# Two blocks of a small language model on one core: pool products moved behind the compressed scores, recurrence outputs turned into four PSUM banks

## Chip, cores and metric

One core of one Trainium2 chip runs the whole program. The metric is device time in microseconds (us), the median of several runs; lower is better. TensorE (PE in the rows, its weight loads PEld) multiplies, VectorE (DVE), ScalarE (ACT) and GpSimd (POOL) work on elements, SyncE (SP) issues most transfers.

## What is computed

A sequence of 512 tokens of width 1024 passes through two blocks, all in fp32. Cut to what matters here:

```python
# first block
u, q, kv, nsa_g, merge_g = split(rms_norm(x) @ w_in)
pooled_g = window_mean(u_g, 2, 4, 8, 16) - u_g               # four groups g of 128 columns
y_pool = concat(pooled_g @ pool_w[g]) * pool_scale @ w_pool_out
kc, vc = compress_blocks(kv)                                 # 31 compressed keys and values
p_cmp = masked_softmax(q @ kc * scale)                       # then attention over all branches
x = x + (gate_pool * y_pool + gate_nsa * y_nsa) @ w_out      # and a gated feed-forward
# second block
o = gated_delta_rule(q, k, v, g, beta)                       # recurrence, 4 heads, 8 chunks of 64 tokens
oa = rmsnorm(o, gdn_norm_w) * silu(z)
ob = chunk_band_attention(qb, kb, vb, rel_bias)
x = x + (sigmoid(ga) * (oa @ w_branch_a) + sigmoid(gb) * (ob @ w_branch_b)) @ w_out
```

## The kernel before, in words

Activations lie transposed in SBUF, features on the 128 partitions, the 512 tokens along the free axis. Every weight tile is a *chunk* of 128 x 1024 values. It is loaded into one of two slots of `w_raw` by SyncE (`load`, L584), cast by ScalarE to `w_hi` (L790), and its rest `w_lo` is made by VectorE or, in the stretches that the change touches, by GpSimd in four pieces (`low_pieces`, L561). A product is then three matmuls of 512 columns for each 128 rows of weights: `w_hi` with `h_hi`, `w_hi` with `h_lo`, `w_lo` with `h_hi` (L1686 to L1688).

The order on each engine is written out by hand; semaphores join the engines. Long serial passages, the compressed attention of block 1 and the recurrence of block 2, give TensorE little to do. Into their gaps the program puts pieces of a projection that is wanted only later: `fill(step, n)` on TensorE runs so many *pieces* (a quarter of a chunk, six matmuls) as a plan gives that step. Two chunks are in PSUM banks 0 and 1 at a time. When a chunk's four pieces are done, VectorE's `serve(step, n)` scales it into `stage` (L1164) and SyncE stores it (L588); ScalarE's and GpSimd's `serve` of the same step make the weights of the chunk two further on. Each engine reaches its `serve` in its own program order. The pieces that matter here:

```python
# step: pieces run by TensorE; VectorE's, ScalarE's and GpSimd's serve of the step runs up to chunk first_piece // 4
compress 3: 24      compress 4: 25      scores 0: 26-29     scores 1: 30-33
out 0: 73-75   out 1: 76-78   out 2: 79-81   out 3: 82-84   turn 0: 85-86   turn 1: 87-88
```

So the last piece of out 3, number 84, is the first of chunk 21. ScalarE casts that chunk in `serve("out", 3)`, which stands behind its loop over the four heads:

```python
for h in range(GH):
    act.wait_ge(f_dve, 4 + 2 * h)
    act.activation(oa_hi[:, h, :], oa[:, h % 2, :], ACT.Copy).then_inc(oa_h, 1)
...
act.wait_ge(oa_l, GH)
act.dma_start(rel[:, :, :], diagonals(rel_dram)).then_inc(rel_loaded, 16)
serve("out", 3)
```

PSUM has eight banks: ACC (0, 1) for filling, BS (2, 3), BT (4, 5), BO (6, 7). In the compressed stage TensorE multiplies four pooled groups by `pool_w`; ScalarE makes `yp_hi` of each (L1009), VectorE `yp_lo` (L1429). Before the change groups 2 and 3 (counted from 0) reuse the banks of groups 0 and 1 and wait for their `yp_lo`; the scores (L1961) follow behind them and one filling piece. In the out stage TensorE transposes four heads of `o_nat` (printed as p2a), 4 transposes a head, through the helper `turn` (L1785) into BT and BT+1 in alternation, so that heads 2 and 3 wait until VectorE has read heads 0 and 1 into `oa` (L1654). VectorE's loop takes one head at a time: two halves of `oa`, a wait for ScalarE's `oa_hi` (L1114), the subtraction `oa_lo` (L1141).

Of the kernel before, what the change touches and what calls it, by code (L numbers as in the profile page):

```python
# [25 lines left out]
ACT = mybir.ActivationFunctionType  # L26
AXX = mybir.AxisListType.X

P = 128
# [8 lines left out]
GH = 4  # L38
# [162 lines left out]
def two_blocks(nc, t_in, out):  # L201
# [10 lines left out]
    with ctx:  # L212
# [54 lines left out]
        p1 = area("p1", [P, 15, T], F32, 0)  # L267
# [8 lines left out]
        pool_w = area("pool_w", [P, 4, P], F32, 82)  # L276
# [20 lines left out]
        yp_hi = area("yp_hi", [P, 4, T], F32R, 0)  # L297
        yp_lo = area("yp_lo", [P, 4, T], F32R, 16)
# [47 lines left out]
        o_nat = p2a[:, 4:8, :].rearrange("p c (h d) -> p c h d", h=GH)  # L346
        o_sq = p2a[:, 8:12, :].rearrange("p c (h d) -> p c h d", h=GH)
        oa = area("oa", [P, 2, T], F32, 34)
# [17 lines left out]

        banks = ctx.enter_context(nc.psum_tensor("banks", [P, 8, T], F32))
        ACC, BS, BT, BO = 0, 2, 4, 6
        POOLED = (BS + 1, BT + 1)

        def bank(n, shape=None):
            v = banks[:, n, :]
            return v.rearrange("p (a b) -> p a b", a=shape) if shape else v
# [58 lines left out]
        pooled = sem("pooled")  # L432
        pool_mul = sem("pool_mul")
        yp_h, yp_l = sem("yp_h"), sem("yp_l")
# [54 lines left out]

        LATE_BANK = (1, 1)  # L490
        KEY_BANK = (BO, BS)

        block = ctx.enter_context(nc.Block())

# [11 lines left out]
        POOL_STEPS = [5 + gi for gi in range(4)]  # L506
# [64 lines left out]
        def wait(eng, s, value):  # L571
            if not isinstance(value, int) or value > 0:
                eng.wait_ge(s, value)
# [211 lines left out]
        def _(act):  # L785
# [218 lines left out]
            act.activation(kc_tmp[:, 1, :], kc_tmp[:, 1, :], ACT.Exp, scale=-0.5).then_inc(c_act, 1)  # L1004
            serve("compress", 3)

            for gi in range(4):
                act.wait_ge(pool_mul, gi + 1)
                act.activation(yp_hi[:, gi, :], bank(POOLED[gi % 2]), ACT.Copy, scale=param("pool_scale", gi, 1))\  # L1009
                    .then_inc(yp_h, 1)  # L1010
            serve("compress", 4)

            act.wait_ge(s_dve, 6)
            act.activation(cmp_s[:, :, :, :, :], cmp_s[:, :, :, :, :], ACT.Exp, scale=DH ** -0.5).then_inc(s_act, 1)
            serve("scores", 0)
            serve("scores", 1)
            act.wait_ge(blk_zero, 1)
            for r in range(8):
# [120 lines left out]
        def _(dve):  # L1139
# [284 lines left out]
            for half in range(2):  # L1424
                dve.tensor_tensor(kc_two[rows(half), half, :], kc_tmp[rows(half), 2, :], kc_tmp[rows(half), 3, :],
                                  ALU.add).then_inc(c_dve, 1)
            for gi in range(4):
                dve.wait_ge(yp_h, gi + 1)
                dve.scalar_tensor_tensor(yp_lo[:, gi, :], bank(POOLED[gi % 2]), param("pool_scale", gi, 1),  # L1429
                                         yp_hi[:, gi, :], ALU.mult, ALU.subtract).then_inc(yp_l, 1)  # L1430
            serve("compress", 4)

            flat = cmp_s[:, :, :, :, :].rearrange("p a b c n -> p (a b c) n")
# [14 lines left out]
            serve("scores", 0)  # L1448
            dve.wait_ge(s_act, 1)
            dve.tensor_reduce(cmp_red[:, 1, :], flat, AXX, ALU.add).then_inc(s_dve, 1)  # L1450
            serve("scores", 1)
            dve.wait_ge(s_dve, 7)
            dve.reciprocal(cmp_red[:, 2, :], cmp_red[:, 1, :]).then_inc(s_dve, 1)
# [192 lines left out]
            def in_pairs(row, side):  # L1646

                return row.rearrange("p (c two t) -> p c two t", c=NT, two=2)[:, :, side, :]

            for h in range(GH):  # L1650
                dve.wait_ge(f_pe, h + 1)
                wait(dve, oa_l, h - 1)
                for side in range(2):
                    dve.scalar_tensor_tensor(in_pairs(oa[:, h % 2, :], side), in_pairs(bank(BT + h % 2), 1 - side),  # L1654
                                             param("gdn_gain"), in_pairs(p2a[:, 12 + h, :], side),
                                             ALU.mult, ALU.mult).then_inc(f_dve, 1)
                dve.wait_ge(oa_h, h + 1)
                sub(oa_lo[:, h, :], oa[:, h % 2, :], oa_hi[:, h, :]).then_inc(oa_l, 1)
                if h == 1:
                    serve("out", 2)  # L1660
# [17 lines left out]
        def _(pe):  # L1678
# [105 lines left out]
            def turn(dst, src, n=P, last=None):  # L1784
                return pe.transpose(dst, src, ident[0:n, 0:n])  # L1785
# [122 lines left out]
                elif n == 2:  # L1908
                    add_parts()
            rotate(5)  # L1910
            pe.wait_ge(c_act, 2)
            for v in range(2):
                for k in range(NT):
                    mm = turn(banks[:, BO + v, k * P:(k + 1) * P], p1[:, VS + v, k * P:(k + 1) * P])
                mm.then_inc(turned[0], 1)
                fill("turn", v)
# [21 lines left out]
            pe.wait_ge(c_act, 3)  # L1938
            pe.matmul(banks[:, BS, 0:NCMP], halves, kc_tmp[:, 0, :], start=True, stop=True).then_inc(c_pe, 1)

            for gi in range(2):
                pe.wait_ge(pooled, sum(POOL_STEPS[:gi + 1]))
                pe.matmul(bank(POOLED[gi % 2]), pool_w[:, gi, :], p1[:, gi, :], start=True, stop=True)\
                    .then_inc(pool_mul, 1)
            fill("compress", 3)
            pe.wait_ge(c_dve, 1)
            pe.matmul(banks[:, BT, 0:NCMP], const("rot"), kc_t[:, :], start=True, stop=True).then_inc(c_pe, 1)
            for gi in range(2, 4):
                pe.wait_ge(pooled, sum(POOL_STEPS[:gi + 1]))
                pe.wait_ge(yp_l, gi - 1)  # L1950
                pe.matmul(bank(POOLED[gi % 2]), pool_w[:, gi, :], p1[:, gi, :], start=True, stop=True)\
                    .then_inc(pool_mul, 1)
            fill("compress", 4)

            pe.wait_ge(c_dve, 5)
            pe.wait_ge(n_sum, 6)
            pe.wait_ge(yp_l, 3)
            for i2 in range(2):
                for n in range(8):
                    i, j, at_ = 2 * i2 + n // 4, n % 4, n * 2 * NCMP  # L1960
                    mm = pe.matmul(banks[:, BS + i2, at_:at_ + 2 * NCMP], p1[:, 4 + j, i * P:(i + 1) * P],  # L1961
                                   kc_two[:, :, :].rearrange("p a b -> p (a b)"), start=True, stop=True)
                mm.then_inc(s_pe, 1)
            fill("scores", 0)
            fill("scores", 1)
            pe.wait_ge(s_dve, 12)
# [118 lines left out]
            for c in range(NCH):  # L2085
# [21 lines left out]
                                   u_new[rs, slot, h, :], start=c == 0 and h == 0, stop=True,  # L2107
                                   skip_group_check=True)
                mm.then_inc(r_o, 1)
            fill("out", 0)  # L2110
            fill("out", 1)
            pe.wait_ge(f_dve, 2)
            for h in range(GH):
                wait(pe, f_dve, 2 * h if h >= 2 else 0)
                for p in range(NT):
                    mm = turn(banks[:, BT + h % 2, p * P:(p + 1) * P], o_nat[:, p, h, :])
                mm.then_inc(f_pe, 1)
            fill("out", 2)
            fill("out", 3)
            for v in range(4):  # L2120
                fill("turn", v)
                pe.wait_ge(qkv_in["v"], 16)
                wait(pe, v_copied[1], v - 1)
                for k in range(NT):
                    mm = turn(banks[:, BO + v % 2, k * P:(k + 1) * P], p2b[:, 8 + v, k * P:(k + 1) * P])
                mm.then_inc(turned[1], 1)
# [130 lines left out]
```

## Time and profile before

| | us |
|---|---|
| median of 3 runs (1584.78 to 1585.86) | 1585.39 |
| the profiled execution's own time | 1585.66 |
| its span, first to last instruction | 1583.9 |
| TensorE busy in the span | 1547.2 |

The rows below come from that one execution; their times count from the start of its span. In a timeline row the first number is the start, the second the duration of the row's instructions together, `x8` their number, and the bracket the idle time of the engine just before with what ended it. Matmuls overlap, so a row's duration is longer than the distance to the next start. The clock column PEclk is the share of 2.4 GHz that was granted: 1.00 is 2.4 GHz, 0.50 is 1.2 GHz.

### The profile page before, as it was taken

What the parts mean: (1) busy time and instruction counts of PE and PEld (TensorE: products, weight loads), DVE (VectorE), ACT (ScalarE), POOL (GpSimd) and SP (SyncE); (2) the same over time, 40 slices, a digit from 0 to 9 for tenths busy, and PEclk for the clock granted to TensorE, in tenths of its full rate; (3) what the DMA queues carried; (4) which work ended last, traced back from release to release, by engine and by line L of the source; (5) the groups of instructions that cost most, each with busy time, mean ns of one, the idle gap of its engine ahead of it and who ended that gap; (6) DMA issues with size and microseconds to landing.
All of it is one profiled execution on the core that took longest, in us unless ns stands there. A gap on an engine that the chain in (4) does not pass through costs nothing.

```text
span 1583.9 us, 21470 instructions
## 1 busy us (share of the span) xinstructions
PE 1547.2 (98%) x7712; PEld 1237.7 (78%) x7712; DVE 896.5 (57%) x1437; ACT 571.4 (36%) x874; POOL 207.8 (13%) x263
## 2 busy tenths in 40 slices
PE   8999999999999999999999999999999999999997
PEld 5876676788888888888787778766788888888885
DVE  6128567565666665333863652346566788887233
ACT  4234456544323333223324413236544332332221
POOL 1548112100000000000002362232100000000000
PEclk9999999999999999999999999999999999999999
DMA  7423112342322323232222241251342232223221
GB/s 245 148 88 107 61 54 72 109 147 93 107 93 93 106 92 114 92 104 77 82 104 99 101 131 54 75 205 67 143 144 94 93 105 94 93 98 121 97 91 71
DMA packets 58100, 164.72 MB, mean 104 GB/s; under 512 B 11936, under 2 KB 12200, under 8 KB 57904
## 3 DMA queue, kind: packets, MB, share of 16 engines
q1 hardware_dynamic: 52784, 158.07, 28.9%
q10 hardware_dynamic: 5248, 5.74, 1.2%
q8 instruction: 43, 0.70, 0.2%
q14 instruction: 25, 0.20, 0.0%
HBM read 148.83 MB, written 14.96 MB: 103 GB/s over the span
## 4 chain that ended last, share of the span: by engine, by line
PE 89%; DVE 5%; DMA 2%; ACT 2%; issue 1%; ACTq 0%; POOL 0%; SPq 0%; DVEq 0%; POOLq 0%
PE banks L1686 26%; PE banks L1688 26%; PE banks L1687 26%; PE banks L1785 2%; PE banks L1796 2%; PE banks L1825 2%; DMA w_raw<-in_w_in 1%; PE banks L2102 0%; PE banks L2081 0%; ACT w_hi L790 0%; PE banks L2093 0%; PE banks L2023 0%; PE banks L2066 0%; DMA w_raw<-in_w_mix 0%; PE banks L1992 0%
## 5 line engine op out<-in xcount | busy, mean ns | idle before, releaser
L1686 PE MATMUL banks<-h_hi,w_hi 128*128 128x512 f32 x1312 | 531.9, 405 | 9.2 <-POOL w_lo L561 4.5
L1688 PE MATMUL banks<-h_hi,w_lo 128*128 128x512 f32 x1312 | 513.3, 391 | 0.0
L1687 PE MATMUL banks<-h_lo,w_hi 128*128 128x512 f32 x1312 | 513.2, 391 | 0.0
L790 ACT ACTIVATE w_hi<-w_raw 128x1024 fp32r<-128x1024 f32 (+1 forms) x226 | 249.3, 1103 | 474.5 <-PE banks L1688 412.6
L1686 PEld LDWEIGHTS banks<-h_hi,w_hi 128*128 128x128 f32 x1312 | 247.6, 189 | 95.9 <-issue 28.9
L1687 PEld LDWEIGHTS banks<-h_lo,w_hi 128*128 128x128 f32 x1312 | 247.8, 189 | 53.3 <-issue 5.1
L1688 PEld LDWEIGHTS banks<-h_hi,w_lo 128*128 128x128 f32 x1312 | 247.3, 188 | 53.0
L553 DVE TENSOR_TENSOR w_lo<-w_raw,w_hi 128x1024 fp32r<-128x1024 f32 (+1 forms) x168 | 217.9, 1297 | 82.6 <-ACT w_hi L790 82.5
L561 POOL TENSOR_TENSOR w_lo<-w_raw,w_hi 128x256 fp32r<-128x256 f32 x232 | 177.3, 797 | 380.2 <-ACT w_hi L790 380.0
L1686 PE MATMUL banks<-act_hi,w_hi 128*128 128x512 f32 x352 | 136.9, 389 | 0.0
L1687 PE MATMUL banks<-act_lo,w_hi 128*128 128x512 f32 x352 | 136.9, 389 | 0.0
L1688 PE MATMUL banks<-act_hi,w_lo 128*128 128x512 f32 x352 | 136.9, 389 | 0.0
L1164 DVE TENSOR_TENSOR t_raw<-banks,rms_inv 128x512 f32<-128x512 f32 x66 | 45.6, 691 | 78.3 <-PE banks L1688 70.9
L1187 DVE TENSOR_TENSOR X<-X,banks 128x512 f32<-128x512 f32 (+1 forms) x32 | 22.0, 687 | 98.6 <-PE banks L1688 98.6
L1686 PEld LDWEIGHTS banks<-act_hi,w_hi 128*128 128x128 f32 x352 | 66.1, 188 | 13.8
L1688 PEld LDWEIGHTS banks<-act_hi,w_lo 128*128 128x128 f32 x352 | 66.1, 188 | 13.7
L1687 PEld LDWEIGHTS banks<-act_lo,w_hi 128*128 128x128 f32 x352 | 66.1, 188 | 13.7
L862 ACT ACTIVATE act_hi<-t_gate 128x512 f32 (+1 forms) x44 | 27.8, 632 | 133.8 <-DVE t_gate L1256 133.8
L895 ACT ACTIVATE at_p<-at_sm,cols 128x128 f32<-128x128 f32 (+2 forms) x96 | 52.9, 552 | 61.3 <-PE banks L1785 42.7
L747 POOL MEMSET x_inv<- 128x2048 f32 x1 | 1.8, 1813 | 518.5 <-DVE p2a L1164 518.5
L859 ACT ACTIVATE t_gate<-t_gate 128x512 f32<-128x512 f32 x44 | 27.9, 633 | 95.1 <-DVE t_gate L1232 95.1
L1686 PE MATMUL banks<-mix_hi,w_hi 128*128 128x512 f32 x128 | 49.8, 389 | 0.0
(291 smaller groups left out, 1739.1 us busy)
## 6 DMA issues: line engine op xcount, KB each, us to landing
w_raw<-in_w_up SPq DMA_DIRECT2D x88, 512.0 KB, 3.5
w_raw<-in_w_fill SPq DMA_DIRECT2D x44, 512.0 KB, 3.5
w_raw<-in_w_down SPq DMA_DIRECT2D x32, 704.0 KB, 4.0
late_scratch<-stage SPq DMA_DIRECT2D x44, 256.0 KB, 2.0
w_raw<-in_w_mix SPq DMA_DIRECT2D x16, 512.0 KB, 4.3
sg<-late_scratch SPq DMA_DIRECT2D x16, 512.0 KB, 3.8
w_raw<-in_w_out SPq DMA_DIRECT2D x16, 512.0 KB, 3.5
w_raw<-in_w_in SPq DMA_DIRECT2D x13, 512.0 KB, 3.5
```

Source lines behind the costliest of these rows:

```text
L553: eng.tensor_tensor(w_lo[:, c.slot, 0:kt * P], w_raw[:, c.slot, 0:kt * P], w_hi[:, c.slot, 0:kt * P], ALU.subtract).then_inc(lo_ready, PIECES)
L561: eng.tensor_tensor(w_lo[:, c.slot, cols], w_raw[:, c.slot, cols], w_hi[:, c.slot, cols], ALU.subtract).then_inc(lo_ready, 1)
L790: act.activation(w_hi[:, c.slot, 0:kt * P], w_raw[:, c.slot, 0:kt * P], ACT.Copy)\
L859: act.activation(t_gate[:, j, :], t_gate[:, j, :], ACT.Silu).then_inc(silu_done[b], 1)
L895: act.activation(a.p[:, s % 2, half, off:off + w], a.sm[:, half, off:off + w], ACT.Exp, bias=a.nbias[:, c:c + 1], scale=DH ** -0.5, accum_ ...
L1164: return dve.tensor_tensor(dst, src, rms_inv[:, :], ALU.mult)
L1686: pe.matmul(dst, w_h, hi[:, kr, :], start=first and n == 0, stop=False)
L1687: pe.matmul(dst, w_h, lo[:, kr, :], start=False, stop=False)
L1688: mm = pe.matmul(dst, w_l, hi[:, kr, :], start=False, stop=last and n == len(ks) - 1)
L1785: return pe.transpose(dst, src, ident[0:n, 0:n])
L1796: mm = pe.matmul(banks[:, BS + half, off:off + w], q_tile(j)[rows(half), i * P:(i + 1) * P], k_tile(j, b)[rows(half), 0:w], start=True, st ...
L1825: mm = pe.matmul(banks[rows(half), BO + j % 2, i * P:(i + 1) * P], v_tile(j, b, half, k), a.pt[u % 2][half][:, off + k * P:off + (k + 1) * P],
```

## The change

In the compressed stage the pool products 2 and 3 go to banks BO and BO+1 of their own, behind the scores, and no longer wait for `yp_lo`; the scores wait for one `yp_lo` instead of three. ScalarE's and VectorE's shares of these two groups move behind the Exp and the sum of the compressed softmax. Before that, the first of the two value turns no longer waits for `hid_t`. In the out stage the four heads are turned into four banks without a wait between them, the filling step out 2 moves in front of the turns, and the value turns that use BO and BO+1 next wait until all heads are read. The order on GpSimd and SyncE, and the plan of pieces, stay.

```diff
-        POOLED = (BS + 1, BT + 1)
+        POOLED = (BS + 1, BT + 1, BO, BO + 1)
+        TURNED = (BT, BT + 1, BO, BO + 1)
...
# ScalarE
-            for gi in range(4):
+            def pooled_high(gi):
                 act.wait_ge(pool_mul, gi + 1)
...
+            for gi in range(2):
+                pooled_high(gi)
             serve("compress", 4)
             act.wait_ge(s_dve, 6)
             act.activation(cmp_s[:, :, :, :, :], cmp_s[:, :, :, :, :], ACT.Exp, scale=DH ** -0.5).then_inc(s_act, 1)
             serve("scores", 0)
+            for gi in range(2, 4):
+                pooled_high(gi)
             serve("scores", 1)
# VectorE
+            for gi in range(2):
+                pooled_low(gi)
             serve("compress", 4)
...
             dve.tensor_reduce(cmp_red[:, 1, :], flat, AXX, ALU.add).then_inc(s_dve, 1)
+            for gi in range(2, 4):
+                pooled_low(gi)
             serve("scores", 1)
...
-                    dve.scalar_tensor_tensor(in_pairs(oa[:, h % 2, :], side), in_pairs(bank(BT + h % 2), 1 - side),
+                    dve.scalar_tensor_tensor(in_pairs(oa[:, h % 2, :], side), in_pairs(bank(TURNED[h]), 1 - side),
# TensorE
-            pe.wait_ge(c_act, 2)
             for v in range(2):
+                if v:
+                    pe.wait_ge(c_act, 2)
...
             pe.matmul(banks[:, BT, 0:NCMP], const("rot"), kc_t[:, :], start=True, stop=True).then_inc(c_pe, 1)
-            for gi in range(2, 4):
-                pe.wait_ge(pooled, sum(POOL_STEPS[:gi + 1]))
-                pe.wait_ge(yp_l, gi - 1)
-                pe.matmul(bank(POOLED[gi % 2]), pool_w[:, gi, :], p1[:, gi, :], start=True, stop=True)\
-                    .then_inc(pool_mul, 1)
             fill("compress", 4)
             pe.wait_ge(c_dve, 5)
             pe.wait_ge(n_sum, 6)
-            pe.wait_ge(yp_l, 3)
+            pe.wait_ge(yp_l, 1)
...
                 mm.then_inc(s_pe, 1)
+            pe.wait_ge(c_act, 4)
+            for gi in range(2, 4):
+                pool_product(gi)
             fill("scores", 0)
             fill("scores", 1)
...
-            fill("out", 0)
-            fill("out", 1)
+            for n in range(3):
+                fill("out", n)
             pe.wait_ge(f_dve, 2)
             for h in range(GH):
-                wait(pe, f_dve, 2 * h if h >= 2 else 0)
                 for p in range(NT):
-                    mm = turn(banks[:, BT + h % 2, p * P:(p + 1) * P], o_nat[:, p, h, :])
+                    mm = turn(banks[:, TURNED[h], p * P:(p + 1) * P], o_nat[:, p, h, :])
                 mm.then_inc(f_pe, 1)
-            fill("out", 2)
             fill("out", 3)
             for v in range(4):
                 fill("turn", v)
                 pe.wait_ge(qkv_in["v"], 16)
+                pe.wait_ge(f_dve, 2 + 2 * GH)
```

## Rows read from the trace of the kernel before

**Rows 1.** The page: engines over the span, then the last chain by engine.

```profile
PE 1547.2 (98%) x7712; PEld 1237.7 (78%) x7712; DVE 896.5 (57%) x1437; ACT 571.4 (36%) x874; POOL 207.8 (13%) x263
...
PE 89%; DVE 5%; DMA 2%; ACT 2%; issue 1%; ACTq 0%; POOL 0%; SPq 0%; DVEq 0%; POOLq 0%
```

**Rows 2.** TensorE's waits over the span: total us, times, longest us.

```profile
PE banks L1951 <- DVE yp_lo L1429: 2.4, 1, 2.4
...
PE banks L1785 <- ACT hid_t L979: 1.3, 1, 1.3
```

**Rows 3.** Three stretches: length, busy us per engine (instructions), clock, DMA share, GB/s.

```profile
29.80:36.62 6.82, 5.87 (x14) 4.61 (x15) 6.07 (x9) 1.50 (x2) 4.07 (x6) 0.50 0.37 113
...
159.46:162.87 3.41, 3.41 (x7) 1.93 (x6) 1.33 (x2) 1.37 (x2) 0.00 (x0) 0.50 0.21 79
...
1036.69:1040.10 3.41, 3.37 (x10) 2.89 (x11) 2.03 (x4) 1.26 (x2) 0.00 (x0) 0.50 0.38 144
```

**Rows 4.** TensorE in order of time, compressed stage.

```profile
152.49 1.96 PE L1943 MATMUL banks<-p,pool_w 128*128 128x512 f32 x4
153.89 0.79 PE L1686 MATMUL banks<-h_hi,w_hi 128*128 128x512 f32 x1
...
155.80 0.41 PE L1947 MATMUL banks<-kc_t,consts 128*128 128x31 f32 x2
158.61 2.92 PE L1951 MATMUL banks<-p,pool_w 128*128 128x512 f32 x4 [2.40 <-DVE yp_lo L1429]
...
163.43 3.68 PE L1961 MATMUL banks<-kc_two,p 128*128 128x62 f32 x32
166.92 0.48 PE L1686 MATMUL banks<-h_hi,w_hi 128*128 128x512 f32 x1
...
177.93 1.03 PE L1785 MATMUL banks<-consts,cmp_s 128*31 128x128 f32 x8
```

**Rows 5.** VectorE in order of time, the same stage.

```profile
157.72 1.41 DVE L1429 SCALAR_TENSOR_TENSOR yp_lo<-banks,params,yp_hi 128x512 fp32r<-128x512 f32 x2
...
174.65 1.69 DVE L1465 TENSOR_TENSOR cmp_s<-cmp_s,cmp_red 128x992 f32<-128x992 f32 x1
```

**Rows 6.** ScalarE in order of time, the same stage.

```profile
154.00 1.25 ACT L1009 ACTIVATE yp_hi<-banks,params 128x512 fp32r<-128x512 f32 x2
...
170.36 1.03 ACT L1014 ACTIVATE cmp_s<-cmp_s 128x992 f32<-128x992 f32 x1 [8.11 <-DVE cmp_s L1141]
```

**Rows 7.** TensorE in order of time, out stage.

```profile
1031.62 0.39 PE L1688 MATMUL banks<-h_hi,w_lo 128*128 128x512 f32 x1
1032.75 1.09 PE L1785 MATMUL banks<-consts,p2a 128*128 128x128 f32 x8 [0.74 <-DVE p2a L1643]
...
1037.50 0.78 PE L1686 MATMUL banks<-h_hi,w_hi 128*128 128x512 f32 x1
...
1045.65 0.39 PE L1686 MATMUL banks<-h_hi,w_hi 128*128 128x512 f32 x1
```

**Rows 8.** All engines in order of time, out stage: casts and low weights.

```profile
1031.40 3.94 POOL L561 TENSOR_TENSOR w_lo<-w_raw,w_hi 128x256 fp32r<-128x256 f32 x4 [3.18 <-ACT w_hi L790]
...
1042.98 1.06 ACT L790 ACTIVATE w_hi<-w_raw 128x1024 fp32r<-128x1024 f32 x1 [1.29 <-DVE oa_lo L1141]
...
1044.12 5.76 POOL L561 TENSOR_TENSOR w_lo<-w_raw,w_hi 128x256 fp32r<-128x256 f32 x8 [8.78 <-ACT w_hi L790]
```

**Rows 9.** VectorE in order of time, out stage.

```profile
1032.61 0.68 DVE L1164 TENSOR_TENSOR stage<-banks,rms_inv 128x512 f32<-128x512 f32 x1
1033.44 0.88 DVE L1654 SCALAR_TENSOR_TENSOR oa<-banks,params,p2a 128x256 f32<-128x256 f32 x2
...
1035.02 0.88 DVE L1141 TENSOR_TENSOR oa_lo<-oa,oa_hi 128x512 fp32r<-128x512 f32 x1 [0.70 <-ACT oa_hi L1114]
...
1041.73 0.69 DVE L1141 TENSOR_TENSOR oa_lo<-oa,oa_hi 128x512 fp32r<-128x512 f32 x1 [0.70 <-ACT oa_hi L1114]
```

**Rows 10.** DMA issues in the out stage: KB each, us to landing.

```profile
rel<-rel_scratch ACTq DMA_DIRECT2D x1, 2048.0 KB, 13.8
```

More of the change, by code:

```diff
@@ L1005, in _ @@
             serve("compress", 3)
-            for gi in range(4):
+            def pooled_high(gi):
                 act.wait_ge(pool_mul, gi + 1)
-                act.activation(yp_hi[:, gi, :], bank(POOLED[gi % 2]), ACT.Copy, scale=param("pool_scale", gi, 1))\
+                act.activation(yp_hi[:, gi, :], bank(POOLED[gi]), ACT.Copy, scale=param("pool_scale", gi, 1))\
                     .then_inc(yp_h, 1)
+            for gi in range(2):
+                pooled_high(gi)
             serve("compress", 4)
@@ L1426, in _, with pooled_low @@
                                   ALU.add).then_inc(c_dve, 1)
-            for gi in range(4):
+            def pooled_low(gi):
                 dve.wait_ge(yp_h, gi + 1)
-                dve.scalar_tensor_tensor(yp_lo[:, gi, :], bank(POOLED[gi % 2]), param("pool_scale", gi, 1),
+                dve.scalar_tensor_tensor(yp_lo[:, gi, :], bank(POOLED[gi]), param("pool_scale", gi, 1),
                                          yp_hi[:, gi, :], ALU.mult, ALU.subtract).then_inc(yp_l, 1)
+            for gi in range(2):
+                pooled_low(gi)
             serve("compress", 4)
@@ L1939, in _, with pool_product @@
             pe.matmul(banks[:, BS, 0:NCMP], halves, kc_tmp[:, 0, :], start=True, stop=True).then_inc(c_pe, 1)
+            def pool_product(gi):
+                pe.wait_ge(pooled, sum(POOL_STEPS[:gi + 1]))
+                pe.matmul(bank(POOLED[gi]), pool_w[:, gi, :], p1[:, gi, :], start=True, stop=True)\
+                    .then_inc(pool_mul, 1)
             for gi in range(2):
-                pe.wait_ge(pooled, sum(POOL_STEPS[:gi + 1]))
-                pe.matmul(bank(POOLED[gi % 2]), pool_w[:, gi, :], p1[:, gi, :], start=True, stop=True)\
-                    .then_inc(pool_mul, 1)
+                pool_product(gi)
             fill("compress", 3)
@@ L1947, in _ @@
             pe.matmul(banks[:, BT, 0:NCMP], const("rot"), kc_t[:, :], start=True, stop=True).then_inc(c_pe, 1)
-            for gi in range(2, 4):
-                pe.wait_ge(pooled, sum(POOL_STEPS[:gi + 1]))
-                pe.wait_ge(yp_l, gi - 1)
-                pe.matmul(bank(POOLED[gi % 2]), pool_w[:, gi, :], p1[:, gi, :], start=True, stop=True)\
-                    .then_inc(pool_mul, 1)
             fill("compress", 4)
@@ L1963, in _ @@
                 mm.then_inc(s_pe, 1)
+            pe.wait_ge(c_act, 4)
+            for gi in range(2, 4):
+                pool_product(gi)
             fill("scores", 0)
```

## The prediction

> **What bounds the kernel.** I read the page first. TensorE is busy 98% of the span and carries 89% of the chain that ended last [rows 1]; no other engine comes near. So a change can only win where TensorE stands still or where its clock is low, and it loses wherever it makes TensorE stand still longer. The second view is TensorE's waits over the whole span: the pool products on L1951 wait 2.4 us for `yp_lo`, and a turn waits 1.3 us for `hid_t` [rows 2]. The third is the granted clock: three stretches at 0.50, that is at 1.2 GHz instead of 2.4. One lies in the start, which the diff leaves alone, one right behind the wait on L1951, one inside the turning of the recurrence outputs [rows 3]. Both later ones lie where the diff works. The fourth view is the order of time on each engine in those two stretches [rows 4 to 10]; there the reader is to see for each gap which instruction ended it, and what had to run before that instruction.
>
> **Unit prices.** Filling matmuls at full clock: 48 run from 166.92 to 177.93 [rows 4], 0.229 us each. A fill piece has six, 1.38 us. At half clock 14 matmuls are busy for 5.87 us [rows 3], 0.42 us each, so each loses 0.19 us: about 1.5 us in a busy stretch of 3.41 us and 2.7 us over the 5.87 us. Two pool products take 1.40 us to the next start, and the first fill behind them is 0.4 us longer than usual [rows 4]: 1.7 us of path.
>
> **Edit 1, the first value turn without its wait.** The 1.3 us wait for `hid_t` [rows 2] goes; everything TensorE issues next up to L1947 moves up by it. What is late next is L1947 at 155.80, which needs `kc_t`, and that stands on VectorE behind `pooling` 2 and 3, which pace themselves. The same 1.3 us therefore come back as a wait in front of L1947. From below this edit is worth nothing; from above it cannot be worth more than 1.3 us. I take 0, because VectorE is busy with the pooling up to `kc_t` and only its small waits for TensorE could close.
>
> **Edit 2, products 3 and 4 behind the scores.** Before: L1947 at 155.80, a gap until the first `yp_lo` is out, products from 158.61 (2.92 us, mostly at half clock), one fill piece at half clock, scores at 163.43, next filling at 166.92 [rows 4]. After: the fill piece "compress 4" runs right behind L1947 (156.0 to 157.4; its weights are the second piece of a chunk whose first piece has just run). The scores then wait for `kc_two` and for one `yp_lo` instead of three. The `yp_lo` pair starts at 157.72 and takes 1.41 us [rows 5], so the first is out at about 158.5, and product 3 did start at 158.61 on just that event [rows 4]. The scores start there, 4.8 us earlier than at 163.43. They take 163.43 to 166.92, 3.5 us; then come both products, 1.7 us, whose new banks BO and BO+1 have been read long before. Filling begins at 158.6 + 3.5 + 1.7 = 163.8 instead of 166.92: **-3.1 us**. In this are 1.2 us of the 2.4 us wait, saved by the fill piece, and the loss of the half-clock stretch. If the clock falls here too, 1.5 us of that go.
>
> Does it last? The compressed turns need the last multiplication into `cmp_s`, which ended at 174.65 + 1.69 = 176.34, while TensorE came at 177.93 [rows 4, 5]: 1.6 us to spare. That chain starts with the scores and so moves up 4.8 us, and gets two insertions: behind the Exp (ending 165.5 + 1.03) ScalarE takes the two `yp_hi`, 1.25 us [rows 6], in front of the weight cast for scores 1; VectorE takes both `yp_lo`, 1.41 us [rows 5], behind the sum. Allowing VectorE its wait for ScalarE, some 0.2 us, it ends near 176.3 - 4.8 + 1.6 = 173.1. TensorE comes at 163.8 + 11.0 = 174.8. Nothing waits. I bound the term by -2.0 (two thirds kept) and -4.0 (0.9 us gained by edit 1 as well).
>
> **Edit 3, the turning of the recurrence outputs.** Before, TensorE finishes filling at about 1031.85, turns heads 0 and 1 at 1032.75, waits for `oa` before heads 2 and 3, and fills again from 1037.50, at half clock until 1040.10 [rows 3, 7]. Six pieces follow: out 2 and out 3. The last of the six opens chunk 21 and starts at 1045.65 [rows 7]. It is the place that decides. Its low weights come from GpSimd at 1044.12, from a ScalarE cast at 1042.98 [rows 8], which ScalarE only reaches behind all four `oa_hi`, behind the wait for all four `oa_lo` and behind the issue of the `rel` DMA. VectorE makes `oa_lo` one head after the other: head 0 from 1033.44, its subtraction from 1035.02, the last head's from 1041.73 to 1042.42 [rows 9]. Four banks don't shorten this: VectorE waits for ScalarE's `oa_hi` inside each head, and that wait stays.
>
> After: the first piece of out 2 runs 1031.85 to 1033.2. The second opens chunk 20, whose bank is free after VectorE's eviction, 1032.61 + 0.68 [rows 9], and whose low weights are under way from 1031.40, four pieces in 3.94 us [rows 8]; so it runs almost without a gap, and the third ends at 1036.05. Only now come the turns. A group of four is read some 0.7 us after it begins (eight began at 1032.75, the first `oa` at 1033.44) [rows 7, 9], so VectorE's chain begins at 1036.7 instead of 1033.44: **3.3 us late**. Head 0's subtraction was 0.2 us longer (0.88 us) than the last one's (0.69 us) [rows 9] and I don't count that again, so the chain ends at 1042.42 + 3.1 = 1045.5. The cast follows at 1046.1, GpSimd 1.14 us later at 1047.2, its first piece (5.76 us for eight, 0.72) at 1047.9 [rows 8]. TensorE has meanwhile turned all heads (16 at 1.09 us for eight: 1.9 us at most, to 1038.0) and run two pieces (to 1040.7). It then **stands still for about 7 us** in front of the piece that opens chunk 21, until 1048.0: **+2.35 us** against 1045.65. The removed waits between 1031.85 and 1037.50 are thus collected in one place and lengthened. Bounds: 2.0 if the turns are read as soon as four of them can be done, 3.0 if the opening of chunk 20 slips by the 0.7 us of a GpSimd piece.
>
> The GpSimd row beside head 0 is where a page bears on the 0.2 us. The `oa_lo` subtraction took 0.88 us there, beside GpSimd's casts, and 0.69 us for the last head [rows 8, 9]. The Trainium skill, "GPSIMD Engine Reference", section "1. Specifications", says that VectorE instructions with two SBUF inputs contend with GpSimd; the trace agrees, and as GpSimd would be through its four pieces before the moved chain begins its subtractions, the term would be 2.35 by that and 2.55 by the row as it stands.
>
> Behind that wait the clock is at half again, as it was after the shorter waits in both stretches and in the start [rows 3]. Price between 1.5 us (one stretch like 1036.69 to 1040.10) and 2.7 us (the start's). A pause of 7 us is nearer to the start's, so I take **+2.3 us**. The Trainium skill, "TensorE: Matmul & The Clock Gate", section "HAM oscillation — how this bites in real kernels", speaks against the change here: bursts of matmuls parted by long waits are slowed at the start of each burst. By it this term stands; without it the sum would be -0.75 us.
>
> What comes behind is moved with TensorE. The `rel` DMA is issued 3.1 us later, at about 1045.6, and landed in 13.8 us [rows 10]: 1059.4. Attention's first mask needs it only behind nine pieces and four value turns, at 1048.0 + 12.4 us or later still, by the half clock and the turns. The slack is small but positive. The added wait of the value turns for ten `f_dve` is over when the last `oa` is, before 1045; two fill pieces lie in between.
>
> **Sum.** -3.1 + 2.35 + 2.3 = +1.55 us on the profiled execution's own 1585.66 us: 1587.2. That execution lies 0.27 us above the median of 1585.39, so I forecast **1586.9 us**. A change within 0.2% (3.2 us) can't be told from none in a measurement of this kernel.
>
> **Rivals.**
> *Forecast (0.66):* gain and loss nearly cancel; terms at their bounds give -4.0 + 2.0 + 1.5 = -0.5 to -2.0 + 3.0 + 2.7 = +3.7, mostly within 0.2%; 0.05 of this is slower.
> *Edit 3 gains too (0.06):* the piece that opens chunk 21 is not held, TensorE goes through at 1040.7, 5 us earlier than before, and the end is at 1585.4 - 3.1 - 5.0 = 1577.3. For it: before, the piece waited for nothing. Against it: its weights were there (1044.84) only 0.8 us before it began, and the cast's place behind the four heads is unchanged.
> *The compressed softmax comes late (0.13), the side of slower:* the `yp` copies inserted on ScalarE and VectorE push the last `cmp_s` behind TensorE's arrival. It decides once they cost 1.7 us more than I allow (173.1 against 174.8); if it eats the 3.1 us, the result is 1585.4 + 4.65 = 1590.0. For it: both engines are strictly serial there. Against it: 4.8 us of head start.
> *The clock falls in the compressed stage as well (0.15):* TensorE still pauses there, in front of L1947 and of the scores. +1.5 us: 1588.4, on the edge of 0.2%; I count 0.04 of it as slower.
>
> So: faster 0.08 (the second rival and 0.02 for what I don't see), slower 0.05 + 0.13 + 0.04 = 0.22, no difference 0.70. The range 1584.0 to 1589.8 leaves out the second rival below and part of the late softmax above.
>
> **What would show it.** Right: scores 4 to 5 us earlier against L1947, no half clock behind them; the largest wait of the page that is new is TensorE's for `w_lo` from GpSimd, about 7 us, right behind the turns, followed by half clock; `oa` chain unchanged in length and 3 us later. Wrong: no such wait, or TensorE waiting in front of the compressed turns, or filling behind the scores not 3 us earlier.

## The result, and the profile after

The change makes the kernel slower: 1594.59 us (median of 5 runs, 1590.88 to 1595.84) against 1585.39 us beside it (5 runs, 1584.59 to 1587.89), ratio 1.0051, 95% interval 1.0038 to 1.0064. That is 9.2 us, where the forecast was +1.5 us and the range ended at 1589.8. (The ratio goes by all executions; the quotient of the two medians would be 1.0058.)

The page of the changed kernel, engines over the span and the last chain by engine, answers to [rows 1]:

```profile
PE 1551.3 (97%) x7712; PEld 1241.4 (78%) x7712; DVE 898.5 (56%) x1437; ACT 571.1 (36%) x874; POOL 207.8 (13%) x263
...
PE 89%; DVE 5%; DMA 2%; ACT 2%; issue 1%; ACTq 0%; POOL 0%; SPq 0%; DVEq 0%; POOLq 0%
```

TensorE is still the bound, and it is busy 4.1 us longer for the same 7712 instructions. So a part of the loss is not waiting but slower matmuls. TensorE's waits in the changed kernel, the two longest (us in total, times, longest), answer to [rows 2]:

```profile
PE banks L1697 <- POOL w_lo L562: 11.7, 3, 7.3
PE banks L1962 <- DVE kc_t L1419: 3.6, 1, 3.6
```

The first was forecast. The second was forecast as 1.3 us. The waits of 2.4 us for `yp_lo` in front of the products and of 1.3 us for `hid_t` are gone. Three stretches of the changed kernel (length, busy us per engine, clock), answering to [rows 3]:

```profile
153.01:159.85 6.84, 3.20 (x14) 2.21 (x13) 6.50 (x13) 1.13 (x2) 4.20 (x4) 0.99 0.20 72
159.85:170.09 10.24, 10.13 (x38) 8.01 (x37) 4.32 (x8) 0.00 (x0) 0.00 (x0) 0.50 0.22 78
1047.31:1057.55 10.24, 5.68 (x14) 4.47 (x15) 2.58 (x5) 2.63 (x3) 5.56 (x8) 0.50 0.79 277
```

In each of the two stages 10.24 us run at 1.2 GHz, where it was 3.41 us before. In the compressed stage TensorE is busy for 10.13 of them, and the clock still stays down.

**Where the 9.1 us of the two spans (1593.0 against 1583.9) arise.** Two distances serve for all kernels below, each read from one profiled execution. The *compressed distance* runs from the moment when TensorE is ready for the first value turn to the first of the compressed turns: 136.32 (137.66 less its wait of 1.34) to 177.93 before, 41.61 us; 136.60 to 181.39 after, 44.79 us. The *out distance* runs from VectorE's multiplication into `p2a` in front of the heads to the first mask of attention: 1030.40 to 1061.71 before, 31.31 us; 1034.07 to 1070.63 after, 36.56 us. So the compressed stage brings +3.18, the out stage +5.25, and everything else together +0.7.

TensorE of the changed kernel in order of time, both stages, answers to [rows 4, 7]:

```profile
136.60 0.60 PE L1796 MATMUL banks<-consts,p 128*128 128x128 f32 x4
...
158.35 0.41 PE L1962 MATMUL banks<-kc_t,consts 128*128 128x31 f32 x2 [3.64 <-DVE kc_t L1419]
...
160.62 7.06 PE L1971 MATMUL banks<-kc_two,p 128*128 128x62 f32 x32
167.47 3.20 PE L1955 MATMUL banks<-p,pool_w 128*128 128x512 f32 x4
...
181.39 1.03 PE L1796 MATMUL banks<-consts,cmp_s 128*31 128x128 f32 x8
...
1039.96 1.91 PE L1796 MATMUL banks<-consts,p2a 128*128 128x128 f32 x16
...
1051.87 0.79 PE L1697 MATMUL banks<-h_hi,w_hi 128*128 128x512 f32 x1 [7.27 <-POOL w_lo L562]
```

The 32 score matmuls take 7.06 us instead of 3.68, all of them at half clock. What made TensorE wait for `kc_t` is read on VectorE and GpSimd. VectorE of the changed kernel in order of time (`pooling` 2 and `kc_t`):

```profile
140.97 3.39 DVE L522 TENSOR_TENSOR pool_pad<-pool_pad 128x512 f32<-128x512 f32 x3
144.40 4.30 DVE L526 TENSOR_SCALAR pool_pad<-pool_pad 128x496 f32<-128x496 f32 x1
...
158.05 0.25 DVE L1419 SCALAR_TENSOR_TENSOR kc_t<-banks,params,kc_tmp 128x31 f32<-128x31 f32 x1
```

GpSimd of the changed kernel over the same time:

```profile
136.49 8.47 POOL L562 TENSOR_TENSOR w_lo<-w_raw,w_hi 128x256 fp32r<-128x256 f32 x8
144.91 3.52 POOL L742 MEMSET pc_t<- 128x4096 f32 x1
```

The same instructions of the kernel before, which no row ahead shows, GpSimd and then VectorE in order of time (the row at 153.58 is the same scaling in `pooling` 3, while GpSimd stands idle):

```profile
136.04 4.11 POOL L561 TENSOR_TENSOR w_lo<-w_raw,w_hi 128x256 fp32r<-128x256 f32 x4
140.94 4.31 POOL L561 TENSOR_TENSOR w_lo<-w_raw,w_hi 128x256 fp32r<-128x256 f32 x4 [0.79 <-ACT w_hi L790]
145.19 3.52 POOL L741 MEMSET pc_t<- 128x4096 f32 x1
```

```profile
143.81 0.84 DVE L525 TENSOR_SCALAR pool_pad<-pool_pad 128x496 f32<-128x496 f32 x1
...
145.31 0.69 DVE L527 TENSOR_TENSOR p<-pool_pad,p 128x512 f32<-128x512 f32 x1
...
146.95 2.04 DVE L519 COPY pool_pad<-p 128x512 f32<-128x512 f32 x1
...
153.58 0.42 DVE L525 TENSOR_SCALAR pool_pad<-pool_pad 128x496 f32<-128x496 f32 x1
...
155.50 0.25 DVE L1413 SCALAR_TENSOR_TENSOR kc_t<-banks,params,kc_tmp 128x31 f32<-128x31 f32 x1
```

Before, the TENSOR_SCALAR of `pooling` 2 (its scaling by 1/w) was through 0.54 us before GpSimd's zeroing of `pc_t` began, and only the COPY that opens `pooling` 3 met it. After, the zeroing has moved 0.28 us forward and the TENSOR_SCALAR 0.59 us back (both counted from the start of their span), and they meet: 4.30 us instead of 0.84. Seen piece by piece, the TENSOR_SCALAR began before the change during the third of GpSimd's four low-weight pieces (143.19 to 144.38) and after it during the last of eight (143.78 to 144.96), right behind which the zeroing stands. Each of the two ends just behind the zeroing (148.70 against 148.43; before 148.99 against 148.71). The rows of the out stage stand further down, with edit 3.

### The profile page after: what moved, and what is told of

Its sections match the earlier page's. It is cut to its first block, busy times and chain, and to the rows that moved or that the text cites. A ratio compares the mean times of both kernels' runs of the same rounds, so it can differ in the third digit from the quotient of the medians.

```text
span 1593.0 us, 21471 instructions
## 1 busy us (share of the span) xinstructions
PE 1551.3 (97%) x7712; PEld 1241.4 (78%) x7712; DVE 898.5 (56%) x1437; ACT 571.1 (36%) x874; POOL 207.8 (13%) x263
## 4 chain that ended last, share of the span: by engine, by line
PE 89%; DVE 5%; DMA 2%; ACT 2%; issue 1%; ACTq 0%; POOL 0%; SPq 0%; DVEq 0%; POOLq 0%
PE banks L1697 26%; PE banks L1699 25%; PE banks L1698 25%; PE banks L1796 2%; PE banks L1807 2%; PE banks L1836 2%; DMA w_raw<-in_w_in 1%; PE banks L2115 0%; PE banks L2094 0%; ACT w_hi L791 0%; PE banks L2106 0%; PE banks L2036 0%; PE banks L2079 0%; PE banks L1971 0%; DVE pool_pad L522 0%
```

## The experiments

The table gives each kernel's median, its ratio to the kernel before run beside it (with the 95% interval), and of the profiled execution the compressed distance, the length of the half-clock stretch in that stage, and the out distance, all in us. The medians of the kernel before beside them were 1585.36 (first four), 1584.90 (next four) and 1584.66 (last two). A median stands for 5 to 12 executions, a distance for one, and whole spans of single executions mislead: that of e1_alone is 1.4 us shorter than that of the kernel before (1582.5 against 1583.9), although its median is longer, because its first value turn happens to come 3.50 us earlier (132.82 against 136.32).

| kernel | median | ratio | compressed | at half clock | out |
|---|---|---|---|---|---|
| before | 1585.39 | | 41.61 | 3.4 | 31.31 |
| after | 1594.59 | 1.0051 [1.0038, 1.0064] | 44.79 | 10.2 | 36.56 |
| e1_alone | 1588.02 | 1.0015 [1.0005, 1.0025] | 44.01 | 6.8 | 31.24 |
| e2_alone | 1582.43 | 0.9986 [0.9977, 0.9995] | 38.59 | 0 | 30.67 |
| e3_alone | 1590.50 | 1.0032 [1.0020, 1.0043] | 41.65 | 3.4 | 36.16 |
| e12 | 1587.27 | 1.0011 [0.9999, 1.0023] | 44.69 | 10.2 | 30.72 |
| e1_late_zero | 1581.63 | 0.9985 [0.9975, 0.9994] | 38.11 | 0 | 30.70 |
| zero_late | 1585.06 | 0.9995 [0.9986, 1.0004] | 41.22 | 3.4 | 30.69 |
| e3_early | 1583.54 | 0.9988 [0.9979, 0.9998] | 41.59 | 3.4 | 29.07 |
| all_mended | 1581.58 | 0.9983 [0.9971, 0.9994] | 36.75 | 0 | 30.40 |
| after_zero_late | 1586.57 | 1.0006 [0.9998, 1.0015] | 40.06 | 6.8 | 35.55 |
| e12_zero_late | 1580.78 | 0.9972 [0.9960, 0.9984] | 36.78 | 0 | 31.30 |

### 1. Each edit alone, and the first two together

**e1_alone**, the kernel before with edit 1:

```diff
-            pe.wait_ge(c_act, 2)
             for v in range(2):
+                if v:
+                    pe.wait_ge(c_act, 2)
```

> The kernel before with edit 1 alone: the first value turn doesn't wait for hid_t. Theory: the wait of 1.3 us goes, but ScalarE's cast and GpSimd's zeroing of pc_t (3.52 us) come a little earlier and now lie over VectorE's TENSOR_SCALAR of pooling 2, which takes over 4 us as in the changed kernel (0.84 before), so kc_t comes about 2 us later and TensorE waits some 3.6 us in front of L1947: +2 to +3.5 us, the upper end if the clock falls for longer. Rival (mine in the prediction): the time comes back as an equal wait, 0 us; the late kc_t of the changed kernel was then the chance of one execution, and kc_t here comes 20 us after the first value turn as before.

Measured: +2.7 us, compressed distance +2.40. VectorE of this kernel in order of time shows the stretched instruction with the two other edits absent; the second fence is TensorE:

```profile
140.62 4.31 DVE L525 TENSOR_SCALAR pool_pad<-pool_pad 128x496 f32<-128x496 f32 x1
```

```profile
154.59 0.53 PE L1948 MATMUL banks<-kc_t,consts 128*128 128x31 f32 x2 [3.66 <-DVE kc_t L1413]
156.86 3.75 PE L1952 MATMUL banks<-p,pool_w 128*128 128x512 f32 x4 [1.73 <-DVE yp_lo L1429]
```

Edit 1 by itself is the source of the wait for `kc_t`.

**e2_alone**, the kernel before with the diff's POOLED, `pooled_high`, `pooled_low` and `pool_product` parts:

```diff
-            for gi in range(2, 4):
...
-                pe.wait_ge(yp_l, gi - 1)
...
             fill("compress", 4)
...
-            pe.wait_ge(yp_l, 3)
+            pe.wait_ge(yp_l, 1)
...
+            for gi in range(2, 4):
+                pool_product(gi)
```

> The kernel before with edit 2 alone: products 3 and 4 behind the scores. Theory: kc_t comes when it did before, TensorE pauses only 1.2 us in front of the scores, the clock stays at full level through the scores, and filling behind them starts 3.1 us earlier: -3 us. Rival: products and scores in this order let the clock fall whatever happened before, scores take some 7 us at half clock as in the changed kernel instead of 3.5: +0.5 to +1 us.

Measured: -2.9 us, compressed distance -3.02. TensorE of this kernel in order of time, then its stretch from 152 to 175:

```profile
156.03 0.41 PE L1960 MATMUL banks<-kc_t,consts 128*128 128x31 f32 x2
...
158.87 3.75 PE L1969 MATMUL banks<-kc_two,p 128*128 128x62 f32 x32 [0.94 <-DVE yp_lo L1434]
162.46 1.94 PE L1953 MATMUL banks<-p,pool_w 128*128 128x512 f32 x4
```

```profile
152.00:175.00 23.00, 22.06 (x108) 16.99 (x107) 16.99 (x28) 6.42 (x10) 7.34 (x10) 1.00 0.27 92
```

The scores start 2.84 us behind the matmul on `kc_t` (7.63 before, [rows 4]), at full clock.

**e3_alone**, the kernel before with TURNED and the moved `fill("out", 2)`:

```diff
-            fill("out", 0)
-            fill("out", 1)
+            for n in range(3):
+                fill("out", n)
...
-                    mm = turn(banks[:, BT + h % 2, p * P:(p + 1) * P], o_nat[:, p, h, :])
+                    mm = turn(banks[:, TURNED[h], p * P:(p + 1) * P], o_nat[:, p, h, :])
...
-            fill("out", 2)
```

> The kernel before with edit 3 alone: four turns into four banks, out 2 in front of them. Theory: TensorE waits about 7.3 us for the low weights of chunk 21 behind two pieces of out 3, and resumes at half clock for 3 to 6 us: +4.6 to +5.5 us. Rival: part of the loss in the changed kernel's out stage comes from the earlier stages' shift (where the DMAs and casts meet); then this one alone costs less than 3 us.

Measured: +5.1 us, out distance +4.85, with the same wait for `w_lo`. TensorE of this kernel in order of time:

```profile
1048.76 0.80 PE L1687 MATMUL banks<-h_hi,w_hi 128*128 128x512 f32 x1 [7.26 <-POOL w_lo L562]
```

**e12**, the change without its TURNED part (the diff of e1_alone and that of e2_alone together).

> Edits 1 and 2 together, out stage as before. Theory (the two act on each other): edit 1's late kc_t makes TensorE wait 3.6 us, the clock falls, and the scores that edit 2 puts right behind keep it at half for longer than one stretch: +2 to +4 us, more than the sum of the two alone (near -1). Rival: the parts add up, -1 us, and the rest of the 9 us comes from the out stage.

Measured: +1.9 us in the median (its interval just reaches no difference), compressed distance +3.08, where the parts add up to 2.40 - 3.02 = -0.62. So in these executions 3.7 us come from having both; in the medians it is 1.9 against 2.7 - 2.9 = -0.2, that is 2.1. The stage of this execution is that of the changed kernel: a wait of 3.65 us, 10.24 us at half clock, and on TensorE:

```profile
161.31 7.06 PE L1970 MATMUL banks<-kc_two,p 128*128 128x62 f32 x32
```

In e1_alone the clock fell as well, but was back up before the scores, which took 3.68 us. Not every execution of e12 is like the profiled one (1588.07 us): of twelve, five lie between 1583.3 and 1584.6 with a mean clock of 0.994 or 0.995, below the kernel before, and seven between 1586.5 and 1591.1 with 0.991 to 0.993. That the first five kept their clock in this stage fits, but no profile shows it. With the 5.1 us of e3_alone the medians add up to 7.0 of the 9.2, within the intervals.

### 2. The zeroing moved

The suspected meeting is undone without touching edit 1: GpSimd zeroes `pc_t` after its low weights for piece compress 4 instead of before them. ScalarE writes into `pc_t` only behind the compressed turns.

```diff
             serve("turn", 2)
+            serve("compress", 4)
             pool.wait_ge(c_pe, 1)
             pool.memset(pc_t[:, :, :], 0.0).then_inc(blk_zero, 1)
-            serve("compress", 4)
```

**e1_late_zero** has edit 1 and this.

> Edit 1 alone, and GpSimd zeroes pc_t behind the casts of compress 4 instead of in front of them. Theory (edit 1's harm is the zeroing meeting VectorE's TENSOR_SCALAR): that instruction is back near 0.84 us instead of 4.31, kc_t comes 2 to 4 us earlier than with edit 1 alone, the 3.66 us wait in front of L1947 shrinks to under 1.5 us, and the time is at or below the kernel before, 0 to -3 us. Rival (the harm comes from the GpSimd casts that now run in one piece of eight): the TENSOR_SCALAR or its neighbours stay long and the time stays near +2.7 us.

Measured: -3.3 us against before, where e1_alone had +2.7. VectorE and GpSimd of this kernel in order of time, then TensorE:

```profile
143.10 0.84 DVE L525 TENSOR_SCALAR pool_pad<-pool_pad 128x496 f32<-128x496 f32 x1
...
151.67 0.25 DVE L1413 SCALAR_TENSOR_TENSOR kc_t<-banks,params,kc_tmp 128x31 f32<-128x31 f32 x1
```

```profile
135.18 8.47 POOL L561 TENSOR_TENSOR w_lo<-w_raw,w_hi 128x256 fp32r<-128x256 f32 x8
...
154.49 3.52 POOL L742 MEMSET pc_t<- 128x4096 f32 x1
```

```profile
155.75 1.96 PE L1952 MATMUL banks<-p,pool_w 128*128 128x512 f32 x4 [2.20 <-DVE yp_lo L1429]
```

The low weights still run without a gap, as in the changed kernel; only the zeroing is elsewhere. The TENSOR_SCALAR is back at 0.84 us, `kc_t` comes 16.4 us after the first turn instead of 21.5 (154.29 less 132.82) in e1_alone, and the wait for it is gone. The zeroing is the cause of that wait, not the casts.

**zero_late** has this alone, without edit 1.

> The kernel before with the later zeroing of pc_t alone. Theory: the copy of pooling 3 (2.04 us before, ending just behind the zeroing) falls to 0.4 to 0.9 us, yp_lo comes about 1 us earlier, and the 2.4 us wait on L1951 shrinks by that: -1 us, or -2.5 if the half-clock stretch behind it goes too. Rival: VectorE loses the same time to GpSimd's casts, which move up in place of the zeroing: 0 us.

Measured: no difference (0.9995). The miss teaches something: the COPY of `pooling` 3 falls from 2.04 to 0.42 us and `kc_t` comes earlier, yet TensorE is held by its own wait for `hid_t` and by `yp_lo` behind `kc_t`, for 2.20 us:

```profile
155.84 3.64 PE L1951 MATMUL banks<-p,pool_w 128*128 128x512 f32 x4 [2.20 <-DVE yp_lo L1429]
```

Of the 3.11 us by which the compressed distance of e1_late_zero is shorter (38.11 against 41.22), 1.40 lie ahead of the matmul on `kc_t` (17.95 against 19.35 us behind the moment when TensorE is ready for the first turn): there the free time on VectorE and the free turn on TensorE are worth something only together. The other 1.71 lie behind it, where both kernels do the same and wait the same 2.20 us. They are the half-clock stretch, which came in this execution and not in that of e1_late_zero. The medians lie 3.4 us apart.

**after_zero_late** is the whole change with this.

> The whole change, with nothing altered but the place of GpSimd's zeroing of pc_t, which goes behind the casts of piece compress 4. Theory (edit 1 lets the zeroing meet VectorE's TENSOR_SCALAR on pool_pad; kc_t comes late, the clock falls, the scores run at half clock): the TENSOR_SCALAR is back at about 0.84 us, no wait of 3.6 us in front of the matmul on kc_t, scores in about 3.7 us at full clock; the out stage keeps its 7 us wait for w_lo. The time falls from 1594.6 to the sum of its parts, -3.3 (edit 1 with the later zeroing) -2.9 (edit 2 alone) +5.1 (edit 3 alone) = -1.1 against before: about 1584.3 us, ratio 0.998 to 1.001. Rival (the loss lies in the three edits together, above all in an out stage that starts at another clock, and the zeroing only in part): the compressed stage mends as said but the time stays at 1589 us or more.

Measured: +1.9 us against before instead of +9.2; 3.0 above the -1.1 of the theory, with a ratio inside the range that it gave, while the rival's 1589 or more lies outside the interval. The one moved line takes away 7.3 of the 9.2 us in the medians. In the profiled executions 4.7 of it are compressed distance (40.06), and 1.0 is the out stage, where the clock stayed low for 6.8 us instead of 10.24. TensorE of this kernel in order of time, then the half-clock stretch:

```profile
157.43 4.84 PE L1971 MATMUL banks<-kc_two,p 128*128 128x62 f32 x32 [0.77 <-DVE yp_lo L1435]
162.06 3.73 PE L1955 MATMUL banks<-p,pool_w 128*128 128x512 f32 x4
```

```profile
159.92:166.70 6.78, 6.78 (x19) 4.52 (x19) 3.48 (x6) 1.18 (x2) 0.00 (x0) 0.50 0.00 0
```

Here the clock fell in the middle of the scores, behind a pause of 0.77 us, and they took 4.84 us for the 3.7 expected. This execution (1589.02 us) is one of the two slowest of twelve; the median is 1586.57.

**e12_zero_late** is edits 1 and 2 with this.

> Edits 1 and 2 with GpSimd's zeroing of pc_t behind the casts of compress 4; the out stage is that of the kernel before. Theory (the parts add where no half clock comes between): -3.3 - 2.9 = -6.2 us against before, about 1579.2 us, ratio 0.995 to 0.997, with scores at full clock in 3.7 us, the compressed turns about 38 us behind the first turn (41.6 before) and no half clock in that stage. Rival (both edits earn the same stall, the wait in front of the products, and only one of them can): no better than 1582, ratio 0.998 or more.

Measured: -3.9 us, the lowest ratio of all (its interval overlaps those of e2_alone, e1_late_zero, e3_early and all_mended), though 2.3 short of the -6.2 expected; the rival's ratio of 0.998 lies within the interval too. With the same pause of 0.77 us as after_zero_late the clock did not fall. TensorE of this kernel in order of time, then its stretch from 152 to 172:

```profile
155.80 3.75 PE L1970 MATMUL banks<-kc_two,p 128*128 128x62 f32 x32 [0.77 <-DVE yp_lo L1434]
159.39 1.94 PE L1954 MATMUL banks<-p,pool_w 128*128 128x512 f32 x4
```

```profile
152.00:172.00 20.00, 19.23 (x99) 15.55 (x98) 13.71 (x22) 3.99 (x6) 8.88 (x9) 1.00 0.24 80
```

Its compressed distance is -4.83 against before, where e1_late_zero (-3.50) and e2_alone (-3.02) add up to -6.52. A reason that fits: both of those lack the half-clock stretch of before, and only one of two edits can save it. Counted once, at the 1.71 us read between zero_late and e1_late_zero, it leaves -4.81. That is argued from the sizes and not tested by a run of its own.

### 3. The cast that opens chunk 21

**e3_early** is edit 3 with two `serve` calls moved, so that ScalarE casts chunk 21 before its loop over the heads and VectorE empties the banks of chunk 19 behind head 0:

```diff
# ScalarE
             serve("out", 1)
+            serve("out", 3)
             for h in range(GH):
# VectorE, in the loop over the heads
-                if h == 1:
-                    serve("out", 2)
-            serve("out", 3)
+                if h == 0:
+                    serve("out", 3)
```

> Edit 3 alone, with ScalarE's cast of chunk 21 in front of its loop over the heads and VectorE's eviction of chunk 19 behind head 0. Theory (the 7.3 us wait is the place of that cast): the wait in front of the piece that opens chunk 21 is gone (under 0.5 us); the next one, at the opening of chunk 22 in turn 1, is 1 to 2.5 us, because its cast still stands behind the loop: -2 to -4 us against the kernel before, -7 to -9 against edit 3 alone. Rival: the wait is set by the later start of the oa chain itself or by the weights' load, and only moves: above 3 us stay in front of chunk 21 and the time is not below the kernel before.

Measured: -1.4 us against before, where e3_alone had +5.1, short of the -2 to -4 expected; out distance 29.07 against 36.16. Chunk 21 opens without a wait. What is late next is shown by TensorE (chunk 22), and by GpSimd and VectorE in front of attention:

```profile
1048.54 0.50 PE L1687 MATMUL banks<-h_hi,w_hi 128*128 128x512 f32 x1 [1.70 <-POOL w_lo L562]
```

```profile
1058.70 0.52 POOL L781 MEMSET rel<- 64x512 f32 x1 [3.58 <-DMA rel<-rel_scratch]
```

```profile
1059.26 0.29 DVE L1271 CUSTOM_DVE_ANT_0 at_sm<-banks,rel 128x128 f32<-128x128 f32 x1 [11.69 <-POOL rel L781]
```

**all_mended** is the whole change with the later zeroing, with these two moves, and with chunk 22 cast behind head 2:

```diff
                 act.activation(oa_hi[:, h, :], oa[:, h % 2, :], ACT.Copy).then_inc(oa_h, 1)
-                if h == 1:
-                    serve("out", 2)
+                if h == 2:
+                    serve("turn", 0)
```

> All three edits, with the later zeroing, the cast of chunk 21 in front of the loop over the heads, that of chunk 22 behind head 2 and the eviction of chunk 19 behind head 0. Theory: -3 us in the compressed stage, about -5 us in the out stage, no stretch at half clock behind the start: -7 to -9 us against the kernel before, some 17 us below the changed kernel. Rival: the half-clock stretches come from the order of products and scores or from the four turns themselves and stay: no better than -4 us.

Measured: -3.3 us, less than half of what was expected. The compressed stage is as good as in e12_zero_late (36.75), but the out distance is only 0.9 us below that of before. VectorE and GpSimd of this kernel in order of time:

```profile
1055.02 0.29 DVE L1276 CUSTOM_DVE_ANT_0 at_sm<-banks,rel 128x128 f32<-128x128 f32 x1 [12.98 <-POOL rel L781]
```

```profile
1054.47 0.52 POOL L781 MEMSET rel<- 64x512 f32 x1 [6.53 <-DMA rel<-rel_scratch]
```

The `rel` load (2 MB, 13.7 us) starts behind all four `oa_lo` and bounds the stage of this kernel: VectorE waits 12.98 us for it in front of attention. TensorE then waits 2.66 us behind VectorE and runs 3.41 us at half clock from 1056.71, where the theory had no such stretch. Starting the load earlier was not tried.

## Why the prediction was wrong

**The step that failed is edit 1: "I take 0, because VectorE is busy with the pooling up to `kc_t`".** It took VectorE's pooling as a fixed length. Its length depends on what GpSimd does beside it. Without the wait for `hid_t` the first value turn came earlier, ScalarE's cast of the next chunk came earlier against everything else (138.68 instead of 139.79), GpSimd lost its gap of 0.79 us, and the zeroing of `pc_t` landed on the TENSOR_SCALAR. Alone that is +2.4 us instead of 0 (e1_alone). The bounds, 0 to -1.3, had the wrong sign and were too narrow on both sides: with the zeroing elsewhere the same edit is worth -3.1 (e1_late_zero against zero_late, 38.11 less 41.22; 1.4 of it the wait itself, 1.7 a half-clock stretch that one of the two executions had).

**Edit 2, -3.1, was right as a mechanism and in size**: -3.0 by itself (e2_alone), scores 158.87 for 158.6 forecast. (Its price of the two products, 1.40 and 0.4 us, makes 1.8 and not 1.7; the term is then -3.0.) In the changed kernel it turned into its opposite. Against e2_alone the changed kernel's compressed distance is 6.20 longer: the scores start 1.71 us later, take 3.26 longer up to the products, and products and filling lose another 1.23. The last two, 4.5 us, are half clock. The prediction let the clock fall there at a price of "1.5 us"; the rival built on it had 0.15 and ended at 1588.4. The price came from the one stretch of [rows 3], and the stretch was three times as long: 10.24 us for 3.41.

**Edit 3 went as described.** With everything 3.67 us later by that time, the forecast moments and the measured ones are: `oa` chain 1040.4 and 1040.60, its end 1049.2 and 1049.39, ScalarE's cast 1049.8 and 1049.95, GpSimd 1050.9 and 1051.09, the piece that opens chunk 21 at 1051.7 and 1051.87. VectorE, ScalarE and GpSimd of the changed kernel in order of time, answering to [rows 8, 9]:

```profile
1034.07 2.29 DVE L1654 TENSOR_TENSOR p2a<-p2a,o_red 128x2048 f32<-128x2048 f32 x1 [0.97 <-ACT o_red L1116]
...
1040.60 0.88 DVE L1665 SCALAR_TENSOR_TENSOR oa<-banks,params,p2a 128x256 f32<-128x256 f32 x2 [3.64 <-PE banks L1796]
...
1048.70 0.69 DVE L1147 TENSOR_TENSOR oa_lo<-oa,oa_hi 128x512 fp32r<-128x512 f32 x1 [0.70 <-ACT oa_hi L1120]
```

```profile
1049.95 2.00 ACT L791 ACTIVATE w_hi<-w_raw 128x1024 fp32r<-128x1024 f32 x2 [1.29 <-DVE oa_lo L1147]
```

```profile
1051.09 5.56 POOL L562 TENSOR_TENSOR w_lo<-w_raw,w_hi 128x256 fp32r<-128x256 f32 x8 [12.04 <-ACT w_hi L791]
```

The wait in front of that piece is 7.27 us for "about 7", and costs 1051.87 - 3.67 - 1045.65 = 2.55 us for 2.35. The 0.2 us are the later start of the `oa` chain, not the subtraction of head 0, which took 0.69 us (at 1042.17) as the prediction had it. The rest of the +5.25, 2.7 us, is half clock for the 2.3 taken, at its upper bound: the 13 filling matmuls behind the wait take 5.67 us to the next start, where the same 13 took 2.95 before. That the places of the `serve` calls behind the heads decide, and not the four banks, is shown by e3_early, which takes the wait away by moving ScalarE's cast and with it VectorE's eviction; the cast alone was not moved. The `rel` load was in time, as forecast: no engine waits for it in the changed kernel.

**The sum.** -3.1 + 2.35 + 2.3 was to be 1.55. Measured in the profiled execution: +3.18 for edits 1 and 2 together instead of -3.1, +5.25 for edit 3 instead of +4.65, +0.7 elsewhere, of which no cause was sought. Of the 7.6 us between forecast (+1.55) and measured spans (+9.1), 6.3 lie in the first term. Of the rivals the late softmax did not occur: TensorE did not wait in front of the compressed turns.

## What to carry to other kernels

When a wait is removed on one engine, list what every other engine now does at another time, and look for long instructions of GpSimd that will lie beside VectorE's copies and scalar operations; the length of a VectorE passage read from a trace holds only for that neighbourhood. Small matmuls that are moved up to stand right behind a wait can run wholly at half clock (here 32 in 7.06 us instead of 3.68), so price a stall together with what follows it and not by the shortest half-clock stretch of the page. An edit worth nothing on paper still deserves its own run: edit 1 was put at 0 and cost 2.7 us alone, and one moved line of GpSimd turned +1.9 us for edits 1 and 2 into -3.9.

## What the runs showed that was not expected

**A GpSimd instruction holds some VectorE instructions to its end, and the zeroing is a long one.** The TENSOR_SCALAR of 128x496 takes 0.42 us while GpSimd is idle (153.58 before), 0.84 us when it begins during a low-weight piece of some 1.2 us, and 4.30 when it meets the zeroing; the COPY takes 0.42, and 2.04 when it meets the zeroing. In all twelve kernels each TENSOR_SCALAR and COPY of `pooling` 2 and 3 that was lengthened ended 0.27 to 0.29 us behind the end of a GpSimd instruction. In the kernel before, a TENSOR_TENSOR (145.31, 0.69 us) and an eviction out of PSUM (146.34, 0.69 us) ran beside the zeroing at their usual length. The Trainium skill, "SBUF — State Buffer", section "SBUF: two separate sides", says that the port pair which VectorE shares with GpSimd is locked for a whole instruction and not split, that VectorE wants it for operations in a two-port mode, and that an operation with two SBUF inputs conflicts only with a GpSimd operation that reads SBUF. The trace agrees: the TENSOR_TENSOR, with two SBUF inputs, was not held by the zeroing, which reads nothing. In which mode the TENSOR_SCALAR and the COPY ran no run here shows. That section of the Trainium skill adds that whoever starts first has the pair. The rows leave open who that is: in the changed kernel the TENSOR_SCALAR's record starts at 144.40, during GpSimd's last low-weight piece and 0.51 us before the zeroing, and the zeroing still went first. In the kernel before it starts at 143.81, during a piece that ends at 144.38, and is through at 144.65, although GpSimd's next piece had started at 144.34.

**The fall of the clock is not a fixed property of a program's order.** Behind the same pause of 0.77 us it fell in after_zero_late and did not in e12_zero_late and all_mended; behind the same 2.20 us it fell in zero_late and did not in e1_late_zero. The kernel before, e1_alone and e12_zero_late had 3.4 us at half clock in the out stage and out distances of 31.2 to 31.3; e2_alone, e12, e1_late_zero and zero_late, with the same out stage, had none in their profiled executions and 30.7. The executions of one kernel spread accordingly: e12_zero_late ran from 1577.9 us (mean clock 0.996 and 0.995 in its two shortest) to 1583.5 (0.993), e12 from 1583.3 (0.995) to 1591.1 (0.991). What decides it in one execution stays open, and so does why e12_zero_late's median gain (3.9) is smaller than that of its profiled execution (6.2 by the spans, 1583.9 less 1577.7, of which 1.0 had arisen before the first value turn).
